# Group norm's last operations on GpSimd, the last input tile inside the first convolution, and its inputs turned in one bank

## The reference, cut to what matters

```python
def _rwkv7(p, lp, s0):
    ...
    y32 = (ys[0] + ys[1]).astype(jnp.float32)
    mean = jnp.mean(y32, axis=-1, keepdims=True)
    var = jnp.mean(jnp.square(y32 - mean), axis=-1, keepdims=True)
    y_n = ((y32 - mean) * lax.rsqrt(var + GN_EPS)).astype(p.dtype).reshape(B, L, D_RWKV)
    y_n = y_n * lp['rwkv_gn_w'] + lp['rwkv_gn_b']
    bonus = jnp.sum(r_h * (0.5 * (ks[0] + ks[1])) * lp['rwkv_r_k'], axis=-1, keepdims=True) * v_h
    g = jax.nn.sigmoid(g_low) @ lp['rwkv_g2']
    y = (y_n + bonus.reshape(B, L, D_RWKV)) * g

def _hyena(p, lp):
    ...
    for n in range(HYENA_ORDER):
        zf = jnp.fft.rfft(z.astype(jnp.float32), n=2 * L, axis=1)
        conv = jnp.fft.irfft(zf * kf[None, :, n], n=2 * L, axis=1)[:, :L].astype(p.dtype)
        z = gates[n] * (conv + lp['hy_skip'][n] * z)

def _mixer(h, lp, s0):
    ...
    merged = jax.nn.sigmoid(g_a) * (y_a @ lp['w_pa']) + jax.nn.sigmoid(g_b) * (y_b @ lp['w_pb'])
    return merged @ lp['w_o'], s_fin
```

## Time and profile before

| | us |
|---|---|
| median of three runs | 2284.32 (2281.78 to 2293.54) |
| the profiled execution | 2289.57 |
| its span in the trace | 2287.8 |
| TensorE busy | 2015.5 |
| VectorE busy | 1135.6 |
| ScalarE busy | 759.8 |
| GpSimd busy | 106.6 |

### The profile page before, as it was taken

One profiled execution on the slowest core, in us unless ns is written; L12 is line 12 of the kernel. 1 busy time (PEld: TensorE's weight loads), 2 busy tenths in 40 slices (PEclk: granted clock), 3 DMA queues, 4 the chain that ended last, 5 costly groups with the idle time before them and its releaser, 6 DMA issues.

```text
span 2287.8 us, 30938 instructions
## 1 busy us (share of the span) xinstructions
PE 2015.5 (88%) x13189; PEld 1709.5 (75%) x13189; DVE 1135.6 (50%) x1458; ACT 759.8 (33%) x924; POOL 106.6 (5%) x161
## 2 busy tenths in 40 slices
PE   6789998898779997788988878789999999999996
PEld 2766666665669986666765657788988989899895
DVE  1635444336665546544444475544545545455454
ACT  1332222324134433322223332343433434343342
POOL 3011000000020000101001000000000000000000
PEclk9869989899989998779898999799999999999998
DMA  9403323324155553221232322246555555555552
GB/s 288 132 27 112 112 75 112 112 84 124 55 161 186 185 200 93 69 74 57 93 94 93 97 88 86 98 129 194 185 175 174 168 193 173 186 168 183 186 164 83
DMA packets 247417, 301.27 MB, mean 132 GB/s; under 512 B 8427, under 2 KB 224080, under 8 KB 247152
## 3 DMA queue, kind: packets, MB, share of 16 engines
q1 hardware_dynamic: 240112, 286.28, 39.1%
q0 software_dynamic: 4192, 11.28, 1.6%
q10 hardware_dynamic: 2976, 1.73, 0.3%
HBM read 297.69 MB, written 1.57 MB: 131 GB/s over the span
## 4 chain that ended last, share of the span: by engine, by line
PE 78%; DVE 12%; ACT 4%; issue 4%; DMA 1%; ACTq 0%; DVEq 0%; SPq 0%
PE PS L665 13%; PE PS L666 12%; PE PS L667 12%; PE PS L708 6%; PE PS L995 5%; PE PS L996 5%; PE PS L997 5%; PE PS L833 2%; ACT WH L1106 2%; PE PS L830 2%; PE PS L783 2%; DVE WL L1387 2%; PE PS L851 1%; DVE WL L1396 1%; DMA WRING<-in_w_ada 1%
## 5 line engine op out<-in xcount | busy, mean ns | idle before, releaser
L665 PE MATMUL PS<-HTH,WH 128*128 128x256 f32 x2448 | 725.1, 296 | 81.2 <-DVE WL L1396 38.0
L1387 DVE TENSOR_TENSOR WL<-WRING,WH 128x2048 fp32r<-128x2048 f32 (+1 forms) x213 | 460.2, 2162 | 533.2 <-ACT WH L1106 530.8
L666 PE MATMUL PS<-HTL,WH 128*128 128x256 f32 x2448 | 707.2, 289 | 0.0
L667 PE MATMUL PS<-HTH,WL 128*128 128x256 f32 x2448 | 706.5, 289 | 0.0
L1106 ACT ACTIVATE WH<-WRING 128x2048 fp32r<-128x2048 f32 (+1 forms) x213 | 385.9, 1812 | 691.6 <-PE PS L667 443.8
L665 PEld LDWEIGHTS PS<-HTH,WH 128*128 128x128 f32 x2448 | 481.3, 197 | 103.8 <-issue 65.2
L666 PEld LDWEIGHTS PS<-HTL,WH 128*128 128x128 f32 x2448 | 482.2, 197 | 1.2 <-issue 0.5
L667 PEld LDWEIGHTS PS<-HTH,WL 128*128 128x128 f32 x2448 | 481.7, 197 | 0.0
L708 PE MATMUL PS<-WRING,CONDT 128*2 128x256 f32 x768 | 197.7, 391 | 5.7 <-DMA WRING<-in_w_ada 4.6
L995 PE MATMUL PS<-WH,AH 128*128 128x512 f32 x440 | 171.8, 391 | 13.9 <-DVE WL L1387 13.9
L996 PE MATMUL PS<-WH,AL 128*128 128x512 f32 x440 | 171.3, 389 | 0.0
(11 more groups left out here) (319 smaller groups left out, 2179.3 us busy)
## 6 DMA issues: line engine op xcount, KB each, us to landing
WRING<-in_exp_w_in SPq DMA_DIRECT2D x80, 1024.0 KB, 5.4
WRING<-in_w_ada SPq DMA_DIRECT2D x48, 1024.0 KB, 5.2
WRING<-in_w_in SPq DMA_DIRECT2D x42, 1024.0 KB, 5.4
WRING<-in_exp_w_out SPq DMA_DIRECT2D x40, 1024.0 KB, 5.0
WRING<-in_ffn_w_in SPq DMA_DIRECT2D x22, 1024.0 KB, 5.1
WRING<-in_ffn_w_out SPq DMA_DIRECT2D x11, 1024.0 KB, 4.9
WRING<-in_w_o SPq DMA_DIRECT2D x8, 1024.0 KB, 5.0
WRING<-in_exp_w_in SPq DMA_DIRECT2D x16, 512.0 KB, 3.8
```

Of the source, the lines that this page charges most:

```text
L665: mm(out, h[:, kb, c], hi[:, kb, :], start=kb == 0, stop=False)
L666: mm(out, h[:, kb, c], lo[:, kb, :], start=False, stop=False)
L667: last = mm(out, s[:, kb, c], hi[:, kb, :], start=False, stop=kb == k - 1)
L1387: tt(WL[:, m % 2, 0:k * w], WRING[:, n % RING, 0:k * w], WH[:, m % 2, 0:k * w].bitcast(F32), ALU.subtract)\
```

## The change

The schedule puts the first turn of z ahead of the filters' spectra and takes tile 21 out of the list. TensorE multiplies tile 21 inside the first convolution, one half behind the forward transforms, the other behind the inverse ones. The split of the tile two places on (the first `pb`) and the read of tile 21 move with it. The first turn puts both groups through one PSUM bank, the second group when ScalarE has copied the first. Of `gn` 3 only the reciprocal stays on VectorE. The product, scale-and-shift, bonus and gate go to GpSimd (`gating`), behind its two filter loads. The bonus gets a place of its own, `BONUS`, and `TMP2` moves. `YAH` is copied in the second convolution, `YAL` subtracted behind its gatings.

```diff
@@ schedule
                   ("filter", l, 0), rest[1][0], ("filter", l, 1), ("gn", l, 2), rest[1][1],
-                  ("filter", l, 2), ("gn", l, 3), ("filter", l, 3), rest[2][0], ("gn", l, 4), rest[2][1],
-                  ("turn_z", l)]
+                  ("turn_z", l), ("filter", l, 2), ("gn", l, 3), ("filter", l, 3)]
...
+        elif what == "conv" and a[1] == 0:
+            tiles.append(("in", a[0], 21, 0))
@@ buffers
-        TMP2 = at(20992, "TMP2", [P, 4, TOK])
+        TMP2 = at(22016, "TMP2", [P, 4, TOK])
+        BONUS = at(4096, "BONUS", [P, 4, TOK])
@@ gpsimd
+            def gating(l):
+
+                pool.wait_ge(ev("gn_rstd"), l + 1)
+                pool.wait_ge(ev("bonus_read"), l + 1)
+                pool.wait_ge(ev("gate_copied"), l + 1)
+                steps(pool.tensor_tensor(YT[:, :, :], YT[:, :, :], TMP2[:, :, :], ALU.mult))
+                steps.wait()
+                for b in range(4):
+                    gw, gb = ROW_AT["gw"] + b, ROW_AT["gb"] + b
+                    steps(pool.tensor_scalar(YT[:, b, :], YT[:, b, :], PT[:, gw:gw + 1], PT[:, gb:gb + 1], ALU.mult, ALU.add))
+                steps.wait()
+                steps(pool.tensor_tensor(YT[:, :, :], YT[:, :, :], BONUS[:, :, :], ALU.add))
+                steps.wait()
+                pool.tensor_tensor(YT[:, :, :], YT[:, :, :], GATE[:, :, :], ALU.mult).then_inc(ev("ya"), 1)
@@ tensor, turn_z and conv
-                pe.wait_ge(act_read, read_no[number["in", l, 21, 0]])
+                pe.wait_ge(act_read, read_no[number["in", l, 20, 0]])
...
+                    bank = g if o else 1 - bank_of[number["in", l, 21, 0]]
+                    if g and not o:
+                        pe.wait_ge(ev("zT"), 4 * l + 1)
...
                 if o:
+                    pe.wait_ge(act_read, read_no[number["in", l, 21, 0]])
                     turn_z(l, o)
...
+                if o == 0:
+                    product(number["in", l, 21, 0], HTH, HTL, 0, 2)
                 for g in range(G):
                     pe.wait_ge(ev("spectrum"), 2 * i + g + 1)
...
+                if o == 0:
+                    product(number["in", l, 21, 0], HTH, HTL, 1, 2)
@@ scalar, conv
                 if o == 0:
+                    make_hi(number["in", l, 21, 0] + 2)
+                    mix(l, 21)
                     copy_z(l, 1)
                 else:
+                    act.wait_ge(ev("ya"), l + 1)
+                    fn(YAH[:, :, :], YT[:, :, :], ACT.Copy).then_inc(ev("ya_hi"), 1)
@@ vector, gn and conv
-                    steps(dve.reciprocal(TMP2[:, :, :], TMP2[:, :, :]))
-                    steps.wait()
-                    steps(tt(YT[:, :, :], YT[:, :, :], TMP2[:, :, :], ALU.mult))
...
-                    tt(YT[:, :, :], YT[:, :, :], GATE[:, :, :], ALU.mult).then_inc(ev("ya"), 1)
+                    dve.reciprocal(TMP2[:, :, :], TMP2[:, :, :]).then_inc(ev("gn_rstd"), 1)
...
+                if o == 0:
+                    make_lo(number["in", l, 21, 0] + 2)
                 for g in range(G):
                     t = slice(g * T, (g + 1) * T)
                     dve.wait_ge(ev("conv_ps"), i * 2 + g + 1)
...
+                if o:
+                    dve.wait_ge(ev("ya"), l + 1)
+                    dve.wait_ge(ev("ya_hi"), l + 1)
+                    tt(YAL[:, :, :], YT[:, :, :], YAH[:, :, :].bitcast(F32), ALU.subtract).then_inc(ev("ya_lo"), 1)
```

More of the change, by code:

```diff
@@ L623, in _ @@
                 pool.dma_start(F3[:, :, :], A["hy_f3"][l].rearrange("k (o n) -> k o n", n=DR)).then_inc(f3_in, 16)
+                gating(l)
                 for w in range(2):
@@ L941, in turn_z @@
                         pe.wait_ge(ev("gated"), 2 * l + g + 1)
+                    bank = g if o else 1 - bank_of[number["in", l, 21, 0]]
+                    if g and not o:
+                        pe.wait_ge(ev("zT"), 4 * l + 1)
                     for b in range(4):
-                        last = pe.transpose(PS[:, g, b * P:(b + 1) * P], HY[:, b, g * T:(g + 1) * T], IDENT[:, :])
+                        last = pe.transpose(PS[:, bank, b * P:(b + 1) * P], HY[:, b, g * T:(g + 1) * T], IDENT[:, :])
                     last.then_inc(ev("zT_ps"), 1)
@@ L1259, in gn @@
                     fn(TMP2[:, :, :], TMP2[:, :, :], ACT.Sqrt).then_inc(ev("gn_root"), 1)
-                elif part == 4:
-                    act.wait_ge(ev("ya"), l + 1)
-                    fn(YAH[:, :, :], YT[:, :, :], ACT.Copy).then_inc(ev("ya_hi"), 1)
             def sine(l, part):
@@ L1282, in copy_z @@
                     act.wait_ge(ev("zT_ps"), 2 * (2 * l + o) + g + 1)
-                    fn(ZT[:, g, :], PS[:, g, :], ACT.Copy).then_inc(ev("zT"), 1)
+                    bank = g if o else 1 - bank_of[number["in", l, 21, 0]]
+                    fn(ZT[:, g, :], PS[:, bank, :], ACT.Copy).then_inc(ev("zT"), 1)
             def conv(l, o):
                 if o == 0:
+                    make_hi(number["in", l, 21, 0] + 2)
+                    mix(l, 21)
                     copy_z(l, 1)
                 else:
+                    act.wait_ge(ev("ya"), l + 1)
+                    fn(YAH[:, :, :], YT[:, :, :], ACT.Copy).then_inc(ev("ya_hi"), 1)
                     for g in range(G):
@@ L1644, in gn @@
                     dve.wait_ge(ev("gn_bonus"), l + 1)
-                    tt(two(TMP[:, :, :]), PS[:, 6:8, :], two(RW[:, 8:12, :]), ALU.mult).then_inc(ev("bonus_read"), 1)
+                    steps.wait()
+                    tt(two(BONUS[:, :, :]), PS[:, 6:8, :], two(RW[:, 8:12, :]), ALU.mult).then_inc(ev("bonus_read"), 1)
                 elif part == 3:
                     dve.wait_ge(ev("gn_root"), l + 1)
-                    steps(dve.reciprocal(TMP2[:, :, :], TMP2[:, :, :]))
-                    steps.wait()
-                    steps(tt(YT[:, :, :], YT[:, :, :], TMP2[:, :, :], ALU.mult))
[L1651 to L1658, removed]
-                    tt(YT[:, :, :], YT[:, :, :], GATE[:, :, :], ALU.mult).then_inc(ev("ya"), 1)
[L1660 to L1663, removed]
+                    dve.reciprocal(TMP2[:, :, :], TMP2[:, :, :]).then_inc(ev("gn_rstd"), 1)
             def sine_argument(bank, c, mark):
@@ L1730, in conv @@
                     steps.wait_for(mark, 2 * l + g + 1)
+                if o:
+                    dve.wait_ge(ev("ya"), l + 1)
+                    dve.wait_ge(ev("ya_hi"), l + 1)
+                    tt(YAL[:, :, :], YT[:, :, :], YAH[:, :, :].bitcast(F32), ALU.subtract).then_inc(ev("ya_lo"), 1)
+                    dve.wait_ge(ev("ya_lo"), l + 1)
                 for g in range(G if o else 0):
@@ L1892, in _ @@
                     make_lo(number["ada", a[0], a[1], 0] + 2)
-                elif what in ("cond", "o", "part", "ada", "turn", "z", "line"):
+                elif what in ("cond", "o", "turn_z", "part", "ada", "turn", "z", "line"):
                     pass
@@ L1897, in _ @@
                      "values": values, "ht": ht, "ht_done": ht_done, "wprep": wprep, "scan": scan,
-                     "gn": gn, "sine": sine, "filter": filt, "turn_z": first_turn, "conv": conv, "merge": merge, "gates": gates,
+                     "gn": gn, "sine": sine, "filter": filt, "conv": conv, "merge": merge, "gates": gates,
                      "resid": resid, "affine": affine, "router": router,
```

3 lines of the change are left out of this document (removed).

## The result

The changed kernel takes 2301.2 us against 2286.9 (medians of nine runs each). The ratio of the means is 1.0054, interval [1.0036, 1.0072]. Forecast were 2291.0 and a range up to 2299; the time lies past it. Compared again with 12 runs of its own the same kernel gave 1.0030 [1.0016, 1.0044], and a third time 1.0044 [1.0030, 1.0059]. So it is slower by 0.3 to 0.5%, 7 to 12 us.

The account below looks back on a forecast made before the run. TensorE was taken to bound the kernel (88% busy). A layer: 4.4 us gained less 3.7 port, 1.4 and 1.46 clock, 1.2 `ya`, 3.4 lost, twice 6.7; 2296.3 less 5.25 gives 2291.0 us, range 2280 to 2299.

Parts of the forecast that it names:

- waits at the port: First convolution: VectorE's two-input operations L1718 and L1719 wait for GpSimd instructions, 3.7 us a layer (ends 0 and 5.7).
- gating: First convolution: VectorE's skip-plus-convolution step, queued behind `pb`'s low part; undisturbed 4.0 us earlier than before, not 13.1.
- second convolution's loss in clock: Its forward transform on TensorE, slowed after 6.1 us idle, loses 1.46 us a layer (ends 0 and 2).
- `ya`'s low part: Second convolution: VectorE's subtraction behind the second gating, ahead of `yb`'s low parts, puts 1.2 us on the path to the merge.
- loss in the stretch, a layer: From the reciprocal's start to ScalarE's first copy of the merged tile: net 3.4 us lost a layer, twice 6.7.
- the passage from the profiled execution to the median: Whole kernel: 2296.3 us for the profiled execution, less 5.25 because the median of three runs lay that far below, gives 2291.0.
- the half clock behind the first hole: First convolution: after TensorE idles 4.7 us, group 1's inverse and the half product lose about 1.4 us (ends 0 and 2).
- The 2.8 us by sharing: VectorE beside GpSimd: if they shared bandwidth, four two-input operations would at most double, 2.8 us instead of 3.7.
- The walk: First convolution's products placed beside GpSimd's operations: group 0's pair loses about 0.8 us, group 1's 0.6 and 2.3, together 3.7.
- Nothing collides: Rival: VectorE comes first at the port or GpSimd falls beside PSUM reads, clock stays up; 3.2 us gained a layer, 2278; chance 0.2.
- The whole cover is won: Rival: `pb`'s parts find their tile early, so the 13.1 us come through less 1.2; 2260 us; chance 0.04.
- GpSimd is the slower kind: Rival: GpSimd's tensor_tensors take 3.25 us and VectorE waits whole ones out; 2295, or 2297 with full clock loss; chance 0.24.

Follow-up runs that it names:

- `warm_holes`: Changed kernel plus ten extra unread transforms a layer, four behind group 0's inverse, six behind tile 21's second half; ratio to before 1.0007, stretch 70.3 us.
- `lo_behind`: Changed kernel with `pb`'s low part behind the first convolution's two gatings, tile 21 read before `pb`'s high part; ratio to before 0.9974, stretch 66.9 us.
- `narrow_pool`: Changed kernel with GpSimd's seven operations one column wide in place of 256; ratio to before 0.9975, stretch 68.0 us.
- `turn_late`: Changed kernel with the first turn of z behind the filters' transforms instead of ahead; ratio to before 1.0040, stretch 74.2 and 74.0 us.
- `rebuilt2`: `rebuilt` with ScalarE's high part of `pb` ahead of `ya`'s high part; ratio to before 0.9890, stretch 58.3 and 58.2 us.
- `rebuilt`: Changed kernel with tile 21 whole ahead of the inverses, GpSimd operations cut to 256, `ya` in first convolution, `pb`'s low part behind `yb`'s last; ratio to before 0.9925.
- `after_third`: Changed kernel without further edit, profiled and compared a third time with the kernel before; ratio 1.0044, stretch 74.0 and 73.7 us.
- `before_again`: Unchanged kernel before, repeated without edit against itself; ratio 1.0009, stretch 70.0 and 70.1 us.

## Why the prediction was wrong

The direction and the mechanism were right, the time was not: 2301.2 lies past 2299, and the forecast's ratio, 1.0029, lies below the interval of 1.0054. Step by step, times after the reciprocal's start:

| step | predicted | measured |
|---|---|---|
| first product (before 20.1) | 7.0 | 7.04 |
| waits at the port | 3.7 | 3.4 |
| products end | 18.2 | 18.0 |
| inverse and half product | 6.2 | 6.9 |
| gating (before 27.5) | 28.7 | 29.3 |
| second convolution's loss in clock | 1.46 | 1.45 |
| `ya`'s low part | 1.2 | 1.2 long, 2.0 when moved |
| loss in the stretch, a layer | 3.4 | 4.1 |

The measured loss in the stretch is the mean of six cases of after (73.8) less that of four of before (69.7). Counted only to TensorE's first product of the merge it is 4.0: before is at 47.1 in all four cases, after at 50.9 to 51.3.

**The step that failed is the end of the sum, the passage from the profiled execution to the median, and one term of the sum was mis-sized.** The passage: I took 5.25 us off, because the profiled execution, 2289.57, lay that far above the median of three runs. All 105 runs of before in the five comparisons have a median of 2288.9 (2280.4 to 2299.3). The profiled execution was an ordinary one, and 0.7 was to be taken off.

The term: for the half clock behind the first hole I took 1.4 us (ends 0 and 2). From the products' end at 564.7 to the tile's end at 571.7 are 6.9 us where full clock needs 4.8: 2.1, past my upper end. `warm_holes`, without that half clock, has its gating 2.1 us earlier. These 0.7 us more make 4.1 a layer out of 3.4, 8.2 us in all, 1.0036; the smaller misses of the table cancel. This is inside the intervals of all three comparisons.

With the term alone the forecast would be 2292.5, with both 2297.1; the 27 runs of after have a median of 2297.7 (2290.0 to 2302.6). The last 4 us up to 2301.2 have no place in the stretch. They fit the scatter between sets of runs, whose cause stays open: of the nine runs six took 2300.3 to 2302.6 us and three 2293.0 to 2293.8, the other two sets have medians of 2295.5 and 2301.0, and over all profiles the start of the span alone went from 543.7 to 555.4 us. I had seen 2281.8 to 2293.5 in three runs and gave the range's upper side 8 us, counted from a base that lay too low. The mean of the three ratios is 1.0043, 9.8 us, against the 8.2 of the stretches; whether these last 1.6 us belong to the change stays open. They do not lie behind the second stretch, where before takes 876.2 us and after 875.4 to 875.5.

**Right, and now shown by an experiment.** That the gating queues behind inverse, half product, high and low part: `lo_behind` starts it where the products end. That a VectorE operation with two SBUF inputs waits out a GpSimd instruction whole: `narrow_pool`. The port rule of the Trainium skill ("SBUF — State Buffer", "SBUF: two separate sides"), a port pair held for a whole instruction, agrees with it. The 2.8 us by sharing are refuted. The 2.35 us taken for a 1024-wide operation are rows of 2.36 and 2.35; the third, 2.67, began while VectorE's L1728 still ran. The walk was right in its size by some luck, for its places were off: group 1's pair lost 3.4 us and not 2.9, and group 0's pair lost nothing, where 0.8 was forecast. Beside that pair it was GpSimd that waited: one of its four tensor_scalars took 1.56 us, the others 0.55. That the early turns keep the clock in the filters' transforms: `turn_late`. That the holes cost clock: `warm_holes`, 3.5 us a layer against the 2.9 of the two terms.

**The rivals.** *Nothing collides* was refuted by the rows of 1.97 and 2.82. *The whole cover is won* was refuted by the hole of 9.09 us; a gain of its size can be had by other edits: `rebuilt2` is 11.5 us a layer below before, against the 11.9 it had. *GpSimd is the slower kind* gave 2295 to 2297 and is refuted by its rows of 2.35, though its time was the nearest.

## What to carry to other kernels

A wait belongs to everything queued behind it: before an operation is moved on one engine, list what its new place puts between it and the next link of the chain on all engines. Here that was 9 us for an operation of 2.2. Work moved to GpSimd beside VectorE should be cut narrow, since each of VectorE's operations with two SBUF inputs may wait for one whole instruction. And where a kernel's own runs spread over 10 us, compare fixed stretches of several profiles, take the base of a forecast from more than three runs, and let its range hold that spread as well.

## What the runs showed of the hardware

- VectorE beside GpSimd: 1.97 and 2.82 us for 0.69 next to GpSimd operations of 2.35 to 2.67 us; 0.80 and 1.21 next to ones a quarter as wide. Beside 256-wide tensor_scalars the pair of group 0 stayed at 0.69, and one of the tensor_scalars took 1.56 us for 0.55. The operations that read PSUM and one SBUF tensor were at 0.68 or 0.69 throughout.
- TensorE's grant fell to 0.55 and 0.50 in the holes of 4.71 and 6.33 us, and the rows behind them were slow. Rows were slow behind 3.96 and, in the merge, behind 3.41 too, but not behind 2.94, 1.31 or 1.29. The hole's length alone does not tell: the filters' transforms were slow with 2.14 us idle ahead and not when two turns lay in them, and a forward transform was slow behind 2.17 us in `rebuilt`. In the merge the same hole of 3.41 us was followed by 2.9 us of half clock once and 6.1 three times. Ten extra transforms a layer made the kernel 3.5 us a layer faster.
- The kernel's first 550 us, the same instructions each time but for the first turn of z, took 543.7 to 555.4 us. The profile of 554.7 (`after_third`) has, in a stretch of 50 us, a grant of 0.83:

```profile
250.00:300.00 50.00, 47.26 (x297) 0.83 0.29 95
```

and the one of 543.7 (`before_again`) in the same 50 us 1.00:

```profile
250.00:300.00 50.00, 47.26 (x334) 1.00 0.27 86
```
